# Eight heads in one wave instead of two waves of four, in the inverse of the third mixer's large chunks

## The chip, the cores and the metric

The program runs on one core of a Trainium2 chip, in one launch. The metric is the device time of that launch in microseconds. TensorE, VectorE (DVE), ScalarE (ACT), GpSimd (POOL) and SyncE (SP) each run an instruction stream of their own and meet at semaphores.

## The reference, cut to what matters

The model is two stacks of layers on 256 tokens of width 1024, batch 1. The second stack has four layers on 272 tokens (16 meta tokens and 256 real ones). Its third layer mixes with a gated delta rule over 8 heads of 128, cut into chunks:

```python
def gdn_chunk(state, inputs):
    ...
    lower = jnp.einsum('bhtd,bhsd->bhts', kb, kh) * jnp.exp(jnp.where(strict, diff, -jnp.inf))
    t_mat = jnp.eye(C, dtype=jnp.float32) + lower
    rhs = jnp.concatenate([vb, kb * jnp.exp(b)[..., None]], axis=-1)
    sol = lax.linalg.triangular_solve(t_mat, rhs, left_side=True, lower=True, unit_diagonal=True)
    u, w = sol[..., :GDN_DV], sol[..., GDN_DV:]
    v_new = u - jnp.einsum('bhcd,bhdv->bhcv', w, state)
    attn = jnp.einsum('bhtd,bhsd->bhts', qh, kh) * jnp.exp(jnp.where(incl, diff, -jnp.inf))
    o = attn @ v_new + (qh * exp(b)) @ state
    new_state = state * exp(b_last) + k_dec^T @ v_new
```

(the last two lines are shortened). What the change touches is the solve with the unit lower triangular `t_mat`.

## The kernel before

The kernel is a list of stages. Each stage has a method for each engine (`tensor`, `vector`, `scalar`, `pool`), and these methods are called in the order of the list, so that every engine has one fully unrolled stream. Semaphores count finished instructions by engine; `mark` names a count and `at` waits for it. There is no planner: the order within a stream is the order of the code.

The mixer runs three chunks of 16, 128 and 128 tokens, one after the other, because each needs the state of the one before. The first is a `GdnChunk`, the two large ones (t = 1 and t = 2, the second one with `last` set) are `GdnSquares`. They build the explicit inverse X of `t_mat` and its transpose XT by doubling the block size, seven levels for 128 rows, from 0 to 6. Levels 0 to 4 stay within the four 32x32 squares on the diagonal. These lie "compactly" in tiles of 128 partitions by 8 heads by 32 columns (`Xd`, `XTd`, `Ud`, `BTd`, `LTd`), and a product is a 32x32 matmul on square q of head h. Levels 5 and 6 join the squares and use other tiles.

A level l from 1 to 4 does three sets of 32 products (8 heads by 4 squares) in fp32:

- BX (L4343): the masked part of L times X, into PSUM banks 0 and 1. ScalarE copies it to `Ud` (L4506).
- XB (L4351): X times that, into banks 2 and 3. VectorE subtracts it from `Xd` (L4454).
- XBX (L4354): the transposed product, into banks 4 and 5. VectorE subtracts it from `XTd` (L4455).

The heads are in two groups, g0 with heads 0 to 3 and g1 with heads 4 to 7, one PSUM bank for each group. `square(bank, g, h, q)` is one product's place in PSUM, `squares(bank, g)` the four heads of a group, 128x128. TensorE's order in a level is BX g0, BX g1, then XB and XBX of g0, then XB and XBX of g1. BX of a group waits for that group's X of the level before, XB for that group's copy on ScalarE.

VectorE has other work in its stream ahead of the subtractions of a level: the mask part of the next level (L4412), and what `between(l)` says: the right side less K S (L4430, level 1), the causal mask of the attention (L4433, level 2), pieces of the output's gate (L4442, in the last chunk). ScalarE has in the last chunk one large square (L4508) behind level 1. GpSimd waits for X of level 4 and then copies squares into the tiles of the later levels (L4480). Level 5 is L4361 (BX) and L4366, L4368; level 6 is L4376 and L4382; L4389 is X times the right side, and L4111, L4112 and L4116 the outputs and the new state.

Of the kernel before, what the change touches and what calls it, by code (L numbers as in the profile page):

```python
# [17 lines left out]
ACT = mybir.ActivationFunctionType  # L18
ALU = mybir.AluOpType
AX_X = mybir.AxisListType.X  # L20

P = 128
# [4275 lines left out]
class GdnSquares(GdnChunk):  # L4298
# [7 lines left out]

    def squares(self, bank, g, rows=slice(0, P), width=32):

        return self.c.ps[rows, bank + g, 0:4 * width].rearrange("p (h t) -> p h t", h=4)

    def tensor(self, pe):
# [25 lines left out]
        for l in range(1, self.SMALL):  # L4337
            pe.wait_ge(self.vector_done, self.dve.at("part", l))
            for g, heads in enumerate(self.GROUPS):
                pe.wait_ge(self.vector_done, self.dve.at("X", l - 1, g))  # L4340
                for h in heads:
                    for q in self.Q4:
                        mm = pe.matmul(self.square(0, g, h, q), m["BTd"][l % 2][R[q], h, :], m["Xd"][R[q], h, :], start=True, stop=True)  # L4343
                mm.then_inc(self.tensor_done, self.pe.mark("BX", l, g))
            if l == 1:
                pe.wait_ge(self.vector_done, self.dve.at("AT0"))
            for g, heads in enumerate(self.GROUPS):
                pe.wait_ge(self.scalar_done, self.act.at("BX", l, g))
                for h in heads:
                    for q in self.Q4:  # L4350
                        pe.matmul(self.square(2, g, h, q), m["XTd"][R[q], h, :], m["Ud"][R[q], h, :], start=True, stop=True)  # L4351
                for h in heads:
                    for q in self.Q4:
                        mm = pe.matmul(self.square(4, g, h, q), m["Ud"][R[q], h, :], m["XTd"][R[q], h, :], start=True, stop=True)  # L4354
                mm.then_inc(self.tensor_done, self.pe.mark("XBX", l, g))

        for g, heads in enumerate(self.GROUPS):
            pe.wait_ge(self.vector_done, self.dve.at("X", 4, g))
# [34 lines left out]
    def vector(self, dve):  # L4393
# [14 lines left out]
        def mask(j):  # L4408
            return m["masks"][:, j, :].unsqueeze(1)
# [11 lines left out]
        for g in range(2):  # L4421
            H = slice(4 * g, 4 * g + 4)
            dve.wait_ge(self.tensor_done, self.pe.at("BX", 0, g))
            dve.tensor_tensor(m["Xd"][:, H], mask(0).to_broadcast([P, 4, 32]), self.squares(0, g), ALU.subtract)               .then_inc(self.vector_done, self.dve.mark("X", 0, g))
# [19 lines left out]
        for l in range(1, self.SMALL):  # L4444
# [5 lines left out]
            for g in range(2):  # L4450
                H = slice(4 * g, 4 * g + 4)
                dve.wait_ge(self.tensor_done, self.pe.at("XBX", l, g))
                dve.wait_ge(self.vector_done, self.dve.at("X", l - 1, g))
                dve.tensor_tensor(m["Xd"][:, H], m["Xd"][:, H], self.squares(2, g), ALU.subtract)  # L4454
                dve.tensor_tensor(m["XTd"][:, H], m["XTd"][:, H], self.squares(4, g), ALU.subtract)                   .then_inc(self.vector_done, self.dve.mark("X", l, g))  # L4455
# [15 lines left out]
    def pool(self, pool):  # L4471
# [5 lines left out]
        pool.wait_ge(self.vector_done, self.dve.at("X", 4, 1))  # L4477
# [5 lines left out]
    def scalar(self, act):  # L4483
# [16 lines left out]
        for l in range(1, self.SMALL + 1):  # L4500
            for g in range(2):
                H = slice(4 * g, 4 * g + 4)
                act.wait_ge(self.tensor_done, self.pe.at("BX", l, g))
                if l > 1:
                    act.wait_ge(self.tensor_done, self.pe.at("XBX", l - 1, g))
                act.activation(m["Ud"][:, H], self.squares(0, g), ACT.Copy).then_inc(self.scalar_done, self.act.mark("BX", l, g))  # L4506
# [427 lines left out]
```

## Time and profile before

| what | value |
|---|---|
| median of 3 runs | 2812.64 us |
| lowest and highest | 2811.88 and 2814.21 us |
| the profiled execution's own time | 2804.15 us |
| its span, first to last instruction | 2802.4 us |
| mean granted TensorE clock, as a share of full speed | 0.961 |
| instructions in the trace | 54962 |
| TensorE matmuls, busy | 2606.0 us |
| VectorE busy | 1930.0 us |
| ScalarE busy | 1503.3 us |
| first large chunk, level 1 to the end of level 4 | from 2098.51 to 2119.19 us |
| second large chunk, the same | from 2145.01 to 2165.82 us |

The profile is of one execution. Its times count from the first instruction. A busy time is the sum over instructions that an engine executes; waits and semaphore instructions are not in it. The granted clock of a window is 1.00 at the full 2.4 GHz and 0.50 at 1.2 GHz. "Issue" as a releaser means that the profile shows nothing for which the engine waited. An fp32 product shows as two matmuls and two weight loads.

### The profile page before, as it was taken

Reading aid. Unit: us, or ns where it says so; the run is one execution under the profiler, and the core shown is the slowest. Engines: PE = TensorE matmul, PEld = TensorE weight load, DVE = VectorE, ACT = ScalarE, POOL = GpSimd, SP = SyncE. Lnnn points to the kernel's source line nnn. Section 1 sums busy time; section 2 is a strip of 40 time slices with the busy share of each in tenths; the row PEclk is TensorE's granted clock in tenths of the full one; section 3 lists DMA queues with packets and bytes.
Section 4 is the critical chain, followed back from the end, with each engine's and each line's share of the span. In section 5 each row is a group of like instructions: output and inputs, shape, how many; then the busy total and the mean of one; then the engine's idle time right before and its main releaser. Section 6 shows DMA issues by size and latency. Waiting matters only on the chain.

```text
span 2802.4 us, 54962 instructions
## 1 busy us (share of the span) xinstructions
PE 2606.0 (93%) x21006; PEld 2308.3 (82%) x21006; DVE 1930.0 (69%) x3476; ACT 1503.3 (54%) x2559; POOL 147.7 (5%) x188
## 2 busy tenths in 40 slices
PE   7988899997988999899899998999986899998999
PEld 5845678886776888698799988999886899997999
DVE  3167489997357999775667865777853577766677
ACT  3256378886356888654533464434742433455442
POOL 0010011100001111100000020000010000000000
PEclk9999989999998999999999999999986899999999
DMA  9281389997417999743255433555630255541553
GB/s 324 94 298 61 143 289 380 377 371 271 150 61 266 366 367 358 248 136 106 76 174 171 159 114 106 176 170 165 187 105 3 91 179 167 165 136 62 180 183 118
DMA packets 286595, 529.05 MB, mean 189 GB/s; under 512 B 14336, under 2 KB 207152, under 8 KB 285888
## 3 DMA queue, kind: packets, MB, share of 16 engines
q1 hardware_dynamic: 275472, 506.06, 52.1%
q0 software_dynamic: 9216, 12.61, 1.4%
q10 hardware_dynamic: 1712, 7.69, 0.7%
q8 instruction: 134, 2.20, 0.3%
q14 instruction: 61, 0.50, 0.1%
HBM read 526.21 MB, written 21.06 MB: 195 GB/s over the span
## 4 chain that ended last, share of the span: by engine, by line
PE 77%; DVE 6%; ACT 5%; issue 3%; DMA 1%; PEldq 0%; DVEq 0%; SPq 0%; ACTq 0%; PEld 0%; POOLq 0%
PE ps L2534 17%; PE ps L3116 6%; PE ps L3117 6%; PE ps L3118 6%; PE ps L2137 4%; PE ps L2139 4%; PE ps L2138 4%; PE ps L3136 3%; PE ps L3138 3%; PE ps L3137 3%; PE ps L2173 2%; PE ps L2174 2%; PE ps L2175 2%; PE ps L617 2%; PE ps L1014 1%
## 5 line engine op out<-in xcount | busy, mean ns | idle before, releaser
L2534 PE MATMUL ps<-H_part,W_hi 128*128 128x272 f32 (+2 forms) x2112 | 470.3, 302 | 23.4 <-DVE H_part L2437 11.8
L2339 DVE TENSOR_TENSOR W_lo<-ring,W_hi 128x1024 fp32r<-128x1024 f32 x376 | 443.6, 1222 | 30.1 <-ACT W_hi L2258 29.2
L3165 ACT ACTIVATE W_hi<-ring 128x1024 fp32r<-128x1024 f32 x264 | 263.1, 1049 | 294.3 <-PE ps L3138 185.7
L3116 PE MATMUL ps<-room_part,W_hi 128*128 128x272 f32 (+1 forms) x1408 | 404.7, 287 | 5.0 <-DVE room_part L2437 5.0
L3117 PE MATMUL ps<-room_part,W_hi 128*128 128x272 f32 (+1 forms) x1408 | 403.6, 287 | 0.0
L3118 PE MATMUL ps<-room_part,W_lo 128*128 128x272 f32 (+1 forms) x1408 | 403.0, 286 | 0.0
L2258 ACT ACTIVATE W_hi<-ring 128x1024 fp32r<-128x1024 f32 x376 | 376.6, 1052 | 33.5 <-PE ps L2139 14.2
L2534 PEld LDWEIGHTS ps<-H_part,W_hi 128*128 128x128 f32 x2112 | 351.4, 191 | 41.4 <-issue 29.1
L2534 PE MATMUL ps<-H_part,W_lo 128*128 128x272 f32 (+2 forms) x1216 | 359.2, 295 | 0.0
L3205 DVE TENSOR_TENSOR W_lo<-ring,W_hi 128x1024 fp32r<-128x1024 f32 x264 | 314.2, 1220 | 10.2 <-ACT W_hi L3165 9.4
L2507 DVE TENSOR_TENSOR W_lo<-ring,W_hi 128x1024 fp32r<-128x1024 f32 x186 | 224.6, 1248 | 117.8 <-ACT W_hi L2499 117.2
L3116 PEld LDWEIGHTS ps<-room_part,W_hi 128*128 128x128 f32 x1408 | 265.2, 188 | 7.8 <-issue 7.1
L3117 PEld LDWEIGHTS ps<-room_part,W_hi 128*128 128x128 f32 x1408 | 265.2, 188 | 0.1
L3118 PEld LDWEIGHTS ps<-room_part,W_lo 128*128 128x128 f32 x1408 | 265.1, 188 | 0.0
L3248 DVE TENSOR_TENSOR X<-X,ps 128x272 f32<-128x272 f32 (+1 forms) x352 | 139.4, 431 | 165.1 <-PE ps L3138 162.7
L2499 ACT ACTIVATE W_hi<-ring 128x1024 fp32r<-128x1024 f32 x186 | 185.8, 1050 | 123.3 <-PE ps L2534 84.0
L2534 PEld LDWEIGHTS ps<-H_part,W_lo 128*128 128x128 f32 x1216 | 232.8, 191 | 3.1
L2137 PE MATMUL ps<-W_hi,A_split_hi 128*128 128x512 f32 x512 | 208.8, 408 | 2.8 <-DVE A_split_lo L2345 2.8
L3136 PE MATMUL ps<-room_part,W_hi 128*128 128x272 f32 (+1 forms) x704 | 201.8, 287 | 4.7 <-DVE X L3248 4.7
L2139 PE MATMUL ps<-W_hi,A_split_lo 128*128 128x512 f32 x512 | 202.3, 395 | 0.0
L3138 PE MATMUL ps<-room_part,W_lo 128*128 128x272 f32 (+1 forms) x704 | 202.1, 287 | 0.0
L2138 PE MATMUL ps<-W_lo,A_split_hi 128*128 128x512 f32 x512 | 202.0, 395 | 0.0
(618 smaller groups left out, 5148.7 us busy)
## 6 DMA issues: line engine op xcount, KB each, us to landing
ring<-in_w_expert SPq DMA_DIRECT2D x128, 1024.0 KB, 7.6
ring<-in_w_down SPq DMA_DIRECT2D x108, 1024.0 KB, 6.3
ring<-in_w_gate_up SPq DMA_DIRECT2D x88, 1024.0 KB, 5.1
ring<-in_w_mod SPq DMA_DIRECT2D x42, 1024.0 KB, 5.2
ring<-in_fox_w_in SPq DMA_DIRECT2D x32, 1024.0 KB, 5.9
ring<-in_gdn_w_in SPq DMA_DIRECT2D x16, 1024.0 KB, 5.9
ring<-in_gla_w_in SPq DMA_DIRECT2D x12, 1024.0 KB, 5.2
ring<-in_w_in_even SPq DMA_DIRECT2D x9, 1024.0 KB, 14.4
```

The source lines that it names most:

```text
L2137: pe.matmul(out, xh, wh[:, k, :], start=(q + k == 0), stop=False)
L2138: pe.matmul(out, xh, wl[:, k, :], start=False, stop=False)
L2139: mm = pe.matmul(out, xl, wh[:, k, :], start=False, stop=(q + k == KC - 1))
L2258: act.activation(self.parts(p)[0][:, W], c.ring[:, g % SLOTS, W], ACT.Copy).then_inc(c.hi_done, 1)
L2339: dve.tensor_tensor(lo, c.ring[:, (self.g0 + p) % SLOTS, W], hi.bitcast(F32), ALU.subtract)\
L2534: mm = pe.matmul(self.out(i), a, b, start=(k == 0 and n_part == 0), stop=(k == KC - 1 and n_part == 2))
L3116: pe.matmul(out, wh[:, k, M], hi, start=(k == 0), stop=False)
L3117: pe.matmul(out, wh[:, k, M], lo, start=False, stop=False)
L3118: mm = pe.matmul(out, wl[:, k, M], hi, start=False, stop=(k == KC - 1))
L3136: pe.matmul(out, wh[:, k, M], ah, start=(k == 0), stop=False)
L3138: mm = pe.matmul(out, wl[:, k, M], ah, start=False, stop=(k == 1))
L3205: dve.tensor_tensor(lo, c.ring[:, (self.g0 + p) % SLOTS, C], hi.bitcast(F32), ALU.subtract)\
```

## The change

In `GdnSquares`, levels 1 to 4, the two groups become one wave. TensorE does BX of all heads behind one wait for X of the level before, then XB of all heads behind one wait for ScalarE, then XBX of all heads; XB and XBX have a mark each. ScalarE copies both banks in one instruction for all eight heads, VectorE subtracts both banks from `Xd` behind the mark of XB and from `XTd` behind that of XBX, each in one instruction. A new helper, `all_squares(bank)`, is the view of two banks. Level 0 keeps its two instructions and has one mark for both. Level 5 keeps its groups, but both wait for the whole X of level 4; so does GpSimd.

```diff
+    def all_squares(self, bank):
+
+        return self.c.ps[:, bank:bank + 2, 0:P].rearrange("p a (h t) -> p a h t", h=4)
+
...
         for l in range(1, self.SMALL):
             pe.wait_ge(self.vector_done, self.dve.at("part", l))
-            for g, heads in enumerate(self.GROUPS):
-                pe.wait_ge(self.vector_done, self.dve.at("X", l - 1, g))
-                for h in heads:
-                    for q in self.Q4:
-                        mm = pe.matmul(self.square(0, g, h, q), m["BTd"][l % 2][R[q], h, :], m["Xd"][R[q], h, :], start=True, stop=True)
-                mm.then_inc(self.tensor_done, self.pe.mark("BX", l, g))
+            pe.wait_ge(self.vector_done, self.dve.at("X", l - 1))
+            for h in range(8):
+                for q in self.Q4:
+                    mm = pe.matmul(self.square(0, h // 4, h, q), m["BTd"][l % 2][R[q], h, :], m["Xd"][R[q], h, :], start=True, stop=True)
+            mm.then_inc(self.tensor_done, self.pe.mark("BX", l))
             if l == 1:
                 pe.wait_ge(self.vector_done, self.dve.at("AT0"))
-            for g, heads in enumerate(self.GROUPS):
-                pe.wait_ge(self.scalar_done, self.act.at("BX", l, g))
-                for h in heads:
-                    for q in self.Q4:
-                        pe.matmul(self.square(2, g, h, q), m["XTd"][R[q], h, :], m["Ud"][R[q], h, :], start=True, stop=True)
-                for h in heads:
-                    for q in self.Q4:
-                        mm = pe.matmul(self.square(4, g, h, q), m["Ud"][R[q], h, :], m["XTd"][R[q], h, :], start=True, stop=True)
-                mm.then_inc(self.tensor_done, self.pe.mark("XBX", l, g))
+            pe.wait_ge(self.scalar_done, self.act.at("BX", l))
+            for h in range(8):
+                for q in self.Q4:
+                    mm = pe.matmul(self.square(2, h // 4, h, q), m["XTd"][R[q], h, :], m["Ud"][R[q], h, :], start=True, stop=True)
+            mm.then_inc(self.tensor_done, self.pe.mark("XB", l))
+            for h in range(8):
+                for q in self.Q4:
+                    mm = pe.matmul(self.square(4, h // 4, h, q), m["Ud"][R[q], h, :], m["XTd"][R[q], h, :], start=True, stop=True)
+            mm.then_inc(self.tensor_done, self.pe.mark("XBX", l))
...
         for g, heads in enumerate(self.GROUPS):
-            pe.wait_ge(self.vector_done, self.dve.at("X", 4, g))
+            if g == 0:
+                pe.wait_ge(self.vector_done, self.dve.at("X", 4))
...
-            for g in range(2):
-                H = slice(4 * g, 4 * g + 4)
-                dve.wait_ge(self.tensor_done, self.pe.at("XBX", l, g))
-                dve.wait_ge(self.vector_done, self.dve.at("X", l - 1, g))
-                dve.tensor_tensor(m["Xd"][:, H], m["Xd"][:, H], self.squares(2, g), ALU.subtract)
-                dve.tensor_tensor(m["XTd"][:, H], m["XTd"][:, H], self.squares(4, g), ALU.subtract)                   .then_inc(self.vector_done, self.dve.mark("X", l, g))
+            dve.wait_ge(self.tensor_done, self.pe.at("XB", l))
+            dve.wait_ge(self.vector_done, self.dve.at("X", l - 1))
+            Xd, XTd = (m[x].rearrange("p (a h) t -> p a h t", a=2) for x in ("Xd", "XTd"))
+            dve.tensor_tensor(Xd, Xd, self.all_squares(2), ALU.subtract)
+            dve.wait_ge(self.tensor_done, self.pe.at("XBX", l))
+            dve.tensor_tensor(XTd, XTd, self.all_squares(4), ALU.subtract).then_inc(self.vector_done, self.dve.mark("X", l))
...
-        pool.wait_ge(self.vector_done, self.dve.at("X", 4, 1))
+        pool.wait_ge(self.vector_done, self.dve.at("X", 4))
...
         for l in range(1, self.SMALL + 1):
-            for g in range(2):
-                H = slice(4 * g, 4 * g + 4)
-                act.wait_ge(self.tensor_done, self.pe.at("BX", l, g))
-                if l > 1:
-                    act.wait_ge(self.tensor_done, self.pe.at("XBX", l - 1, g))
-                act.activation(m["Ud"][:, H], self.squares(0, g), ACT.Copy).then_inc(self.scalar_done, self.act.mark("BX", l, g))
+            if l < self.SMALL:
+                act.wait_ge(self.tensor_done, self.pe.at("BX", l))
+                act.activation(m["Ud"].rearrange("p (a h) t -> p a h t", a=2), self.all_squares(0), ACT.Copy)\
+                   .then_inc(self.scalar_done, self.act.mark("BX", l))
+            else:
+                for g in range(2):
+                    H = slice(4 * g, 4 * g + 4)
+                    act.wait_ge(self.tensor_done, self.pe.at("BX", l, g))
+                    act.activation(m["Ud"][:, H], self.squares(0, g), ACT.Copy).then_inc(self.scalar_done, self.act.mark("BX", l, g))
```

## Rows read from the trace of the kernel before

**Rows 1.** The page: span, and busy time of TensorE

```profile
span 2802.4 us, 54962 instructions
...
PE 2606.0 (93%) x21006; PEld 2308.3 (82%) x21006; DVE 1930.0 (69%) x3476; ACT 1503.3 (54%) x2559; POOL 147.7 (5%) x188
```

**Rows 2.** Windows over the levels: busy by engine, clock, DMA share, GB/s

```profile
2098.51:2119.19 20.68, 12.32 (x785) 11.08 (x784) 6.91 (x20) 2.38 (x9) 0.00 (x0) 0.58 0.02 5
...
2145.01:2165.82 20.81, 11.29 (x785) 10.02 (x784) 7.98 (x25) 3.50 (x10) 0.00 (x0) 0.67 0.01 4
```

**Rows 3.** Waits of the whole kernel: us in total, times, longest

```profile
PE ps L4354 <- issue: 11.6, 7, 2.1
...
PE ps L4343 <- issue: 4.6, 3, 1.8
```

**Rows 4.** Timeline at stops: start us, us, operation, count [idle before]

```profile
2100.81 0.17 PEld L4354 LDWEIGHTS ps<-room 32*32 32x32 f32 x6
...
2147.42 0.79 PEld L4343 LDWEIGHTS ps<-room 32*32 32x32 f32 x57 [0.20 <-DVE room L4455]
...
2150.97 0.32 PEld L4354 LDWEIGHTS ps<-room 32*32 32x32 f32 x25
...
2153.54 0.33 PE L4354 MATMUL ps<-room 32*32 32x32 f32 x7 [2.14 <-issue]
```

**Rows 5.** Windows from one resume to the next, five of nine

```profile
2102.18:2106.02 3.84, 1.51 (x128) 1.31 (x129) 1.96 (x4) 0.55 (x2) 0.00 (x0) 0.75 0.02 4
...
2113.01:2117.12 4.11, 2.23 (x127) 1.96 (x128) 0.48 (x2) 0.55 (x2) 0.00 (x0) 0.50 0.02 4
...
2117.12:2120.60 3.48, 2.49 (x129) 2.22 (x129) 0.97 (x4) 0.55 (x2) 1.22 (x4) 0.50 0.02 5
...
2150.07:2153.54 3.47, 1.33 (x128) 1.22 (x128) 0.48 (x2) 0.28 (x1) 0.00 (x0) 0.76 0.02 5
...
2161.14:2164.88 3.74, 1.93 (x128) 1.79 (x128) 0.48 (x2) 0.28 (x1) 0.00 (x0) 0.50 0.02 4
```

**Rows 6.** DMA queues in the window 2144 to 2168

```profile
q8 instruction: 7, 0.11, 1.8%
```

**Rows 7.** A window with one transfer of that queue

```profile
2150.90:2151.30 0.40, 0.40 (x58) 0.39 (x46) 0.35 (x2) 0.00 (x0) 0.00 (x0) 1.00 0.15 41
```

**Rows 8.** Durations by line: ns min/median/max, first and last start, forms

```profile
L4506 ACT ACTIVATE room<-ps x20: 277/277/279, 2099.2 to 2166.5; 128x128 f32<-128x128 f32 x20
...
L4284 ACT ACTIVATE room<-ps x6: 586/597/597, 2074.3 to 2174.9; 128x512 f32<-128x512 f32 x4, 16x512 f32<-16x512 f32 x2
...
L4454 DVE TENSOR_TENSOR room<-room,ps x16: 286/289/289, 2100.8 to 2165.3; 128x128 f32<-128x128 f32 x16
...
L4403 DVE TENSOR_TENSOR H<-ps,room x2: 1225/1225/1225, 2088.8 to 2139.1; 128x1024 f32<-128x1024 f32 x2
```

**Rows 9.** Timeline of level 1 in the second chunk

```profile
2145.01 0.75 PE L4343 MATMUL ps<-room 32*32 32x32 f32 x64
...
2145.54 0.57 ACT L4506 ACTIVATE room<-ps 128x128 f32<-128x128 f32 x2 [2.56 <-PE ps L4343]
...
2145.93 0.34 PEld L4351 LDWEIGHTS ps<-room 32*32 32x32 f32 x29 [0.28 <-issue]
...
2146.21 0.40 PEld L4354 LDWEIGHTS ps<-room 32*32 32x32 f32 x28
```

**Rows 10.** Timeline of the end of level 4, second chunk

```profile
2165.28 0.29 DVE L4454 TENSOR_TENSOR room<-room,ps 128x128 f32<-128x128 f32 x1 [2.41 <-PE ps L4354]
...
2165.49 0.28 DVE L4455 TENSOR_TENSOR room<-room,ps 128x128 f32<-128x128 f32 x1
...
2165.82 0.48 PE L4361 MATMUL ps<-room,H 32*32 32x32 f32 x10 [0.27 <-DVE room L4455]
...
2166.51 0.28 ACT L4506 ACTIVATE room<-ps 128x128 f32<-128x128 f32 x1 [0.64 <-PE ps L4361]
```

**Rows 11.** A window behind the levels of the first chunk

```profile
2119.00:2128.00 9.00, 8.02 (x109) 7.66 (x110) 2.10 (x7) 3.27 (x9) 1.56 (x4) 0.50 0.01 2
```

More of the change, by code:

```diff
@@ L4423, in vector @@
             dve.wait_ge(self.tensor_done, self.pe.at("BX", 0, g))
-            dve.tensor_tensor(m["Xd"][:, H], mask(0).to_broadcast([P, 4, 32]), self.squares(0, g), ALU.subtract)               .then_inc(self.vector_done, self.dve.mark("X", 0, g))
+            ins = dve.tensor_tensor(m["Xd"][:, H], mask(0).to_broadcast([P, 4, 32]), self.squares(0, g), ALU.subtract)
+        ins.then_inc(self.vector_done, self.dve.mark("X", 0))
         dve.tensor_tensor(m["AT"], self.psv(2), m["U"], ALU.mult).then_inc(self.vector_done, self.dve.mark("AT0"))
```

## The prediction

> **What bounds the kernel now.** I read the page first. The program is one core's long chain of matmuls: TensorE is busy 93% of the span and most of the time lies in dense projections that this change does not touch [rows 1]. The third mixer's two large chunks are a small stretch of it. The windows over their inverse levels, from the first product of level 1 to the first products of level 5, come next: 20.68 us in the first chunk (t = 1) and 20.81 us in the second (t = 2), together 41.5 us or 1.5% of the span [rows 2]. To be seen there: the two stretches last the same, though the granted clock is 0.58 in one and 0.67 in the other, and TensorE is busy only 12.3 and 11.3 us of each. Neither TensorE's speed nor its work sets this time.
>
> The list of waits says what does. Over the whole kernel TensorE has idle time that it spends waiting for nothing that the profile shows ("issue"), 11.6 us in 7 pieces before L4354 and 4.6 us in 3 before L4343, and both lines belong to these levels [rows 3]. The pieces are up to 2.1 us long, and they fall inside a row of matmuls of one line where no wait stands: 25 of 32 weight loads of L4354 go out at 2150.97, the other 7 with their matmuls at 2153.54 [rows 4]. So a semaphore cannot be what is missing.
>
> The next view fixes it. Cut the time at the moments at which TensorE goes on after such a piece (I call them resumes): each stretch holds 128 weight loads and 128 matmuls, within one or two missing records, whatever they are and at either clock, and lasts 3.47 to 4.11 us, though TensorE is busy for 1.3 to 2.5 us of it [rows 5], which shows five of the nine. An fp32 product is two matmuls and two loads here (the 32 of BX show as 64 [rows 9]). In the window 2144 to 2168 an "instruction" queue has 7 transfers of 0.11 MB together, so 16 KB each, which is 64 bytes for each of 256 instructions, and one is seen in the window from 2150.90, 0.8 us behind the resume at 2150.07 and over 2 us ahead of the next at 2153.54 [rows 5 to 7]. I read this as instruction fetch: a block of 256 TensorE instructions is asked for when the block before it is entered, and can run some 3.5 us later. A block of long matmuls hides that. A block of 32x32 matmuls, 0.0134 us apart at half clock, is eaten in 1.93 us when nothing waits (the stretch from 2161.14; with a last matmul of 0.24, since 7 take 0.33 [rows 4, 5]), and then TensorE stands.
>
> The Trainium skill says the contrary of this (Runtime: NRT & Kernel Launch, Instruction fetch mechanics): the next page of 256 instructions is fetched during the current one, and that is hidden because issue is slower than the fill. This trace does not agree [rows 4 to 7]: the block size is the same, the hiding is not. By that rule the gaps would be something else and the waits between engines would decide, which is the second rival below.
>
> **The change, part by part.** The level l = 1 to 4 was BX (g0, g1), XB and XBX of g0, XB and XBX of g1, each 16 products; it becomes BX of all 32, XB of all 32, XBX of all 32.
>
> TensorE's instructions: 96 products a level before and after, at the same tiles and sizes. Of the waits, those for the mask part and for X stand on one semaphore and the trace shows no instruction of their own for them. So I take TensorE's count of instructions, and with it the places of the block borders in its stream, as unchanged; the fetch prices them at 3.47 to 4.11 us a block, mean 3.68 over the five stretches of the first chunk from 2102.18 to 2120.60, and 3.70 over the four of the second from 2150.07 to 2164.88 [rows 5].
>
> ScalarE: two evictions of 128x128 at 0.277 us become one of 128x256. Between 0.277 for 128 and 0.597 for 512 elements [rows 8] a straight line gives 0.277 + 0.320 x 128/384 = 0.384 us. Saved 0.17 us a level, 1.4 us over eight. VectorE: four subtractions (0.29 and 0.28 us, starting 0.2 us apart [rows 8, 10]) become two of 128x256, each by the line from 0.289 (128) to 1.225 us (1024) [rows 8]: 0.289 + 0.93 x 128/896 = 0.42 us. A pair of groups took 2 x (0.2 + 0.28) = 0.96 and takes 0.84: saved 0.12 a level, 1.0 us over eight. Bounds for the wide form over two banks, which no row shows: not below one narrow one, 0.28, and not above two, 0.56. Eight waits of 21 ns go with them; nothing is queued behind. All of this lies under the fetch: it is worth 0 as long as a block's own time stays under 3.47 us.
>
> What it adds is exposed waiting. Before, ScalarE evicted g0 while TensorE did BX of g1, and VectorE did g0 during the products of g1. Now TensorE stops for the whole trip twice a level. ScalarE's trip: last matmul 0.24, start 0.07 (g0's half of the 64 ends about 2145.47, its eviction starts at 2145.54), eviction 0.38, weight load 0.12 (2145.82 to 2145.93 [rows 9]), 0.81 us. VectorE's trip: 0.24 + 0.07 + 0.42 + 0.05 (2165.77 to 2165.82 [rows 10]) = 0.78 us, the subtraction from Xd being hidden under XBX. A block that holds both trips needs 1.69 (128 pairs to the last start: 1.93 less 0.24) + 0.81 + 0.78 = 3.28 us, under the shortest stretch, 3.47. By counting 192 pairs a level from the observed borders, three of the nine blocks hold both trips (cover left 0.2 us each), and the others one (cover 1 us) but the last of the first chunk, which has level 5's eviction too and is worked out below. If that cover is gone, the excess is paid in full: with both trips 0.3 us dearer it would be 3 x 0.1 us. I take 0 for it, and up to +1 for the range.
>
> The first chunk: its first border of the levels lies at pair 166 of 192 in level 1 (6 loads into g1's XBX at 2100.81 [rows 4]: 64 + 3 x 32 + 6), so the block before it is entered at pair 38, in BX, ahead of any wave that changes. So its resumes stay, up to the last at 2120.60, which lies in level 5's products behind all of the change. The new order reaches that border sooner than 2120.60: resume at 2117.12, 26 + 64 pairs to 2118.4, VectorE's trip to 2119.1, level 5's first 32 pairs and an eviction to 2120.0. Its 0.77 us gap shrinks to 0.6. Sum of the chunk: 0.
>
> The second chunk: its first resume is 2150.07, in BX of level 2 at pair 57 [rows 4], so its block is entered 128 pairs earlier, at pair 121 of level 1: in XBX of g0 before, at about 2146.46 (24 loads behind 2146.21 [rows 9]), which is 3.6 us before the resume, and this is the length of a fetch again. Afterwards pair 121 is the 57th of XB, and XB waits for the whole wave: BX ends at 2145.76, ScalarE 2145.83 to 2146.21, first load 2146.33, 57th pair 0.54 us later: 2146.87. So the block is entered 0.4 us later, and every resume of this chunk with it: +0.4. At its end, 7 pairs behind the last resume, 0.33 us lie from the resume to the last of them, as before; then one wide subtraction (0.42) stands where two narrow ones took 0.49, and level 5, whose g0 used to go ahead of X of g1 (only g1's waits until 2165.82 [rows 10]), starts as one piece after it. ScalarE's second eviction then queues behind its first: 2165.82 + 0.4 - 0.1 for the first products, + 0.5 to the first eviction, + 0.28 to the second, + 0.28 to its end, against 2166.51 + 0.28 before, 0.69 behind the first products: +0.6 in all for the chunk, against +0.4 from the entry alone. GpSimd's copies, which wait for X of level 4, come at the same offset, and L4389, which waits for the last, starts 3 us behind it. I take +0.5.
>
> Sum: 0 + 0.5 = +0.5 us. The profiled execution took 2804.15 us (span 2802.4 and 1.75 around it), so 2804.65; the median of the three runs shown, 2812.64, lies 8.49 us above it, and nothing here bears on that difference: **2813.1 us**.
>
> **Rivals.**
> 1. Wide instructions gain (faster side). The Trainium skill (VectorE: DVE Perf Modes, The TRN2 errata) says that a fixed cost is paid per instruction, so that few wide ones win. As a mechanism here: if the idle time were the engines' own instruction time, the 1.4 + 1.0 us saved above would come off: 2810.2. If in addition the gaps came from having two waves, and half of the 16.2 us went [rows 3], 8.1 more: 2802.1. For it: the time is spent idle, not in work. Against: the gaps stand inside rows of matmuls with no wait. 3% for the large one; the small one, 5%, is still within no change.
> 2. Lost overlap is paid (other side). If the gaps are not tied to a count of instructions, or grow with the level, TensorE's idle time in each level is the two trips without the last matmuls' own 0.24, 0.57 + 0.54, against the 0.27 us for which it waited for VectorE before [rows 10]: 0.84 us more, eight times 6.7: 2819.3. It decides from where a trip costs over 0.2 us more than I priced it. For it: nothing in the rows shows how the fetch behaves with long waits inside a block. 7%.
> 3. The clock. The granted clock is 0.75 and 0.76 in the stretches from 2102.18 and 2150.07 and 0.50, the lower level, in the last stretch of both chunks [rows 5]. The dense products behind the levels are what pays: 8.0 us busy at 0.50 in the first chunk, of which full clock would take off up to 4 [rows 11], and what follows at the upper level would pay as much if the rise came later. A rise that moves by 3 us costs or gives about 3. For it: the idle pieces move within the blocks. Against: their count and sum hardly change. 11%, half to each side: 2810 to 2816.
> 4. The change does nothing: the end of each chunk is as before, 2812.6. 10%.
>
> **How the numbers follow.** The forecast (2812.2 to 2814.2 by the spread of its terms) has 64%, rivals as given. A measurement of this kernel can tell about 0.2%, 5.6 us, from no change. Faster by more: the large part of rival 1 and a little of the clock, 4%. Slower by more: rival 2 and a little of the clock, 8%. Within: 88%. The range leaves out both large rivals and holds the clock's cases: 2809.0 to 2817.0.
>
> **What the profile of the changed kernel would show.** The resumes still 128 pairs and 3.5 to 4.1 us apart, issue gaps inside rows of matmuls and shorter by the new waits; the first chunk's levels 20.7 us again; the second's about 21.2; ScalarE's eviction near 0.38 and VectorE's subtraction near 0.42 us, eight and sixteen of them; the transfers of the instruction queue as many as before. It is wrong if the distance between resumes changes with the waves: longer by a trip, the fetch starts on something other than the entry of a block; shorter, the gaps were waits.

## The result, and the profile after

The changed kernel took 2813.99 us (median of 12 runs, 2810.12 to 2818.24) against 2806.85 us for the kernel before (12 runs, 2802.81 to 2814.21). The ratio is 1.0023 with a 95% interval of 1.0013 to 1.0032, so by the ratio the change made the kernel slower by 6.4 us (3.6 to 9.0). Run again later, beside 32 new runs of the kernel before, its ratio was 1.0005 (0.9993 to 1.0017), +1.4 us (-2.0 to +4.8). The two intervals share the stretch from +3.6 to +4.8 us. The totals of one kernel spread over 10 us from run to run, so the levels are read from the traces below, and the totals stand beside them.

The page of the changed kernel, the span and the busy times of the engines:

```profile
span 2809.2 us, 54914 instructions
...
PE 2608.6 (93%) x21006; PEld 2311.0 (82%) x21006; DVE 1928.8 (69%) x3460; ACT 1501.8 (53%) x2551; POOL 147.5 (5%) x188
```

TensorE's count of matmuls and loads is the same and its busy time grew by 2.6 us, while the span grew by 6.8 us [rows 1].

The windows over the levels of the changed kernel (length, busy time and count for each engine, granted clock, DMA share, GB/s). The first two reach from the first BX of level 1 to the first product of level 6, the last two only to the first product of level 5:

```profile
2100.80:2126.10 25.30, 15.06 (x849) 13.15 (x849) 6.79 (x14) 2.35 (x7) 1.56 (x4) 0.56 0.01 4
...
2152.13:2176.10 23.97, 13.56 (x850) 11.86 (x849) 8.24 (x19) 3.41 (x8) 1.80 (x4) 0.64 0.02 4
...
2100.80:2123.61 22.81, 12.73 (x770) 11.14 (x769) 6.40 (x12) 1.53 (x4) 0.00 (x0) 0.57 0.02 4
...
2152.13:2173.97 21.84, 11.47 (x769) 9.97 (x768) 7.47 (x17) 2.59 (x5) 0.00 (x0) 0.65 0.02 4
```

The same windows of the kernel before, and two that begin at BX of level 0 and are needed further down:

```profile
2098.52:2121.62 23.10, 13.95 (x849) 12.47 (x849) 7.30 (x22) 3.04 (x11) 1.56 (x4) 0.57 0.02 4
...
2145.01:2167.41 22.40, 12.75 (x849) 11.29 (x848) 8.93 (x27) 4.09 (x12) 1.40 (x3) 0.65 0.02 5
...
2091.29:2121.62 30.33, 18.42 (x928) 16.60 (x929) 9.91 (x28) 6.50 (x25) 1.56 (x4) 0.60 0.02 4
...
2141.58:2167.41 25.83, 15.48 (x928) 13.79 (x928) 11.53 (x33) 5.49 (x18) 1.40 (x3) 0.70 0.02 5
```

From BX of level 1 to level 6 the first chunk went from 23.10 to 25.30 us and the second from 22.40 to 23.97: +2.2 and +1.6, together +3.8 us. To level 5 it was 22.81 and 21.84 us where [rows 2] have 20.68 and 20.81. The second profile of the changed kernel has 25.55 and 24.30 us, +2.45 and +1.90, together +4.35. Both sums lie in what the two intervals of the total share. The profiles differ as much elsewhere: the first chunk's levels begin 2.3 us later in the changed kernel's, and the stretch from them to the second chunk's is another 2.6 us longer, with a lower granted clock. Neither place runs changed work. The second of them, in the kernel before and in the changed kernel:

```profile
2121.62:2145.01 23.39, 19.74 (x216) 18.97 (x216) 10.50 (x32) 8.09 (x20) 0.43 (x1) 0.86 0.01 2
...
2126.10:2152.13 26.03, 22.39 (x216) 21.61 (x217) 10.48 (x32) 8.08 (x20) 0.43 (x1) 0.77 0.01 2
```

The same 216 matmuls are busy 2.65 us longer at 0.77 than at 0.86, which is the whole difference.

TensorE's idle time without a visible releaser, of the whole changed kernel (total, times, longest):

```profile
PE ps L4357 <- issue: 4.8, 4, 1.8
...
PE ps L4353 <- issue: 3.5, 3, 1.3
...
PE ps L4346 <- issue: 3.3, 3, 1.2
```

With [rows 3] beside it: 11.6 us of such gaps in 10 pieces where 16.2 us in 10 pieces stood before. The gaps did shrink. The levels grew all the same, so the gaps are no account of what can be gained.

The stretches from one resume to the next, as in [rows 5]:

```profile
2104.39:2109.24 4.85, 2.46 (x127) 2.09 (x128) 1.89 (x3) 0.38 (x1) 0.00 (x0) 0.50 0.01 3
...
2109.24:2113.27 4.03, 2.23 (x128) 1.99 (x127) 1.18 (x3) 0.00 (x0) 0.00 (x0) 0.50 0.01 4
...
2113.27:2117.02 3.75, 2.24 (x129) 1.97 (x129) 0.42 (x1) 0.38 (x1) 0.00 (x0) 0.50 0.02 4
...
2117.02:2121.60 4.58, 2.46 (x127) 2.09 (x128) 0.42 (x1) 0.38 (x1) 0.00 (x0) 0.50 0.02 4
...
2161.25:2165.91 4.66, 2.38 (x127) 2.03 (x128) 1.34 (x5) 0.38 (x1) 0.00 (x0) 0.50 0.02 4
...
2169.63:2173.10 3.47, 2.15 (x128) 1.89 (x129) 0.42 (x1) 0.38 (x1) 0.00 (x0) 0.50 0.02 5
```

Each still holds 128 pairs of load and matmul, within a missing record. But three of the nine (there are five in the first chunk and four in the second) are 4.85, 4.58 and 4.66 us long, and the others are 3.47 to 4.03. What is special about the three is in the timeline of the first of them:

```profile
2104.39 0.50 PEld L4357 LDWEIGHTS ps<-room 32*32 32x32 f32 x26 [1.29 <-issue]
...
2105.06 0.42 DVE L4460 TENSOR_TENSOR room<-room,ps 128x256 f32<-128x256 f32 x1 [1.72 <-PE ps L4357]
...
2105.60 0.97 PEld L4346 LDWEIGHTS ps<-room 32*32 32x32 f32 x64 [0.71 <-DVE room L4460]
...
2106.76 0.38 ACT L4508 ACTIVATE room<-ps 128x256 f32<-128x256 f32 x1 [4.78 <-PE ps L4346]
...
2107.20 0.75 PE L4353 MATMUL ps<-room 32*32 32x32 f32 x37 [0.49 <-ACT room L4508]
...
2109.24 0.58 PE L4353 MATMUL ps<-room 32*32 32x32 f32 x26 [1.29 <-issue]
```

The block is entered at 2104.39 and its first 26 pairs go out. Then TensorE waits for VectorE, and BX of level 2 starts at 2105.60. A transfer of the instruction queue, some 1.0 to 1.6 us behind the entry in the other blocks, is seen only in the window from 2106.70:

```profile
2106.70:2107.10 0.40, 0.01 (x2) 0.00 (x0) 0.25 (x1) 0.34 (x1) 0.00 (x0) 0.50 0.15 41
```

Narrower windows put its start between 2106.85 and 2106.90. That is 2.5 us behind the entry, 1.3 us behind the first load after the wait (2105.60), and 2.4 us ahead of the resume at 2109.24. The wait for X is an instruction of its own in TensorE's sequencer, the part of the engine that passes instructions on. Of two waits that the code puts ahead of one instruction, the later one shows so in these traces; the other shows no instruction and is, by this reading, attached to the weight load. The wait for X is an instruction of its own in the kernel before too, where it waits for the first group alone and ends early. The line of that wait in the changed kernel, and in the kernel before (times, duration, first and last start):

```profile
L4343 PEldq EVENT_SEMAPHORE  x8: 51/51/51, 2097.3 to 2167.6; - x8
```

```profile
L4340 PEldq EVENT_SEMAPHORE  x8: 51/51/51, 2094.9 to 2158.0; - x8
```

The first chunk's +2.2 us is all in these stretches. The second chunk's +1.6 is not: its four stretches take 15.87 us where four took 14.81, and 3.00 us lie between its last resume (2173.10) and level 6 where 2.53 did (from 2164.88), +0.5 for the end of the levels. The kernels below that make X in one wave have 2.96 to 3.01 us there, also where no stretch is long, and those that keep its groups 2.50 to 2.54 (but for the run with fewer pairs, whose last resume lies elsewhere). So this part belongs to the change and not to the long stretches. What remains is 0.04 us at its start.

### The profile page after: what moved, and what is told of

Read it like the earlier page. It is cut to its first block, busy times and chain, and to the rows that moved or that the text cites. A ratio compares the mean times of both kernels' runs of the same rounds, so it can differ in the third digit from the quotient of the medians.

```text
span 2809.2 us, 54914 instructions
## 1 busy us (share of the span) xinstructions
PE 2608.6 (93%) x21006; PEld 2311.0 (82%) x21006; DVE 1928.8 (69%) x3460; ACT 1501.8 (53%) x2551; POOL 147.5 (5%) x188
## 4 chain that ended last, share of the span: by engine, by line
PE 77%; DVE 6%; ACT 5%; issue 3%; DMA 1%; DVEq 0%; PEldq 0%; SPq 0%; ACTq 0%; POOLq 0%; PEld 0%
PE ps L2534 18%; PE ps L3116 6%; PE ps L3117 6%; PE ps L3118 6%; PE ps L2137 4%; PE ps L2139 4%; PE ps L2138 4%; PE ps L3136 3%; PE ps L3138 3%; PE ps L3137 3%; PE ps L2173 2%; PE ps L2174 2%; PE ps L2175 2%; PE ps L617 2%; PE ps L997 1%
```

## The experiments

The figures for the levels are the time from the first BX of level 1 to the first product of level 6. The stretches and the starts of transfers below are read from each run's trace, the same way as above. Theory W says that the request for the next block of instructions is held while TensorE's sequencer stands at a wait of its own; theory T says that the exposed trips to ScalarE and VectorE cost by themselves.

| kernel | levels, first chunk | second chunk | ratio of the total (95%) |
|---|---|---|---|
| before | 23.10 | 22.40 | 1 |
| changed | 25.30 | 23.97 | 1.0023 (1.0013 to 1.0032) |
| changed, again | 25.55 | 24.30 | 1.0005 (0.9993 to 1.0017) |
| changed, waits in the other order | 23.39 | 22.71 | 1.0015 (1.0000 to 1.0030) |
| changed, one wait less | 23.86 | 22.96 | 1.0006 (0.9991 to 1.0022) |
| before, late wait | 24.15 | 23.53 | 1.0003 (0.9987 to 1.0019) |
| before, BX twice | 31.30 | 30.03 | 1.0056 (1.0037 to 1.0074) |
| BX wave alone | 23.07 | 22.77 | 0.9999 (0.9989 to 1.0010) |
| X wave alone | 25.10 | 23.44 | 1.0014 (1.0004 to 1.0024) |
| before, one wait less | 23.09 | 22.63 | 0.9991 (0.9982 to 1.0001) |

**The waits in the other order.** The changed kernel with one edit:

```diff
-            pe.wait_ge(self.vector_done, self.dve.at("part", l))
             pe.wait_ge(self.vector_done, self.dve.at("X", l - 1))
+            pe.wait_ge(self.vector_done, self.dve.at("part", l))
```

> The changed kernel with the two waits ahead of BX in levels 1 to 4 in the other order (X first, then the mask part). Same instructions, same count. In the changed kernel the wait for X is an instruction of its own at TensorE's sequencer, 8 times, and the stretches between resumes that begin shortly before it are 4.0 to 4.8 us where the others are 3.5 to 4.0. Theory W (the request for the next block of instructions cannot go out while the sequencer stands at a wait of its own; a wait attached to a weight load does not hold it): now the wait for the mask part, long fulfilled, is the one of its own, all stretches are 3.5 to 4.1 us again, and the time from the first BX of level 1 to the first product of level 6 falls from 25.3 and 24.0 us (first and second chunk) to about 23.1 and 22.9. Theory T (a block's own time with two trips in it decides, whichever way it waits): nothing moves, 25.3 and 24.0 within 0.5.

Measured: 23.39 and 22.71 us. With the same instructions in number and kind, 1.9 of the 2.2 us and 1.3 of the 1.6 us are gone. Windows over both chunks' levels, over two stretches, and one with a transfer:

```profile
2096.29:2119.68 23.39, 15.03 (x849) 13.03 (x849) 6.79 (x14) 2.36 (x7) 1.56 (x4) 0.57 0.02 4
...
2143.45:2166.16 22.71, 13.59 (x850) 11.80 (x849) 8.24 (x19) 3.42 (x8) 1.80 (x4) 0.66 0.02 4
...
2100.13:2103.70 3.57, 2.45 (x129) 2.05 (x129) 1.89 (x3) 0.38 (x1) 0.00 (x0) 0.50 0.02 5
...
2103.70:2107.05 3.35, 2.23 (x129) 1.96 (x128) 1.18 (x3) 0.00 (x0) 0.00 (x0) 0.50 0.02 5
...
2101.30:2101.70 0.40, 0.40 (x32) 0.40 (x36) 0.40 (x2) 0.00 (x0) 0.00 (x0) 0.50 0.15 41
```

The timeline of the block that took 4.85 us in the changed kernel, entered here at 2100.13:

```profile
2100.13 0.50 PEld L4357 LDWEIGHTS ps<-room 32*32 32x32 f32 x26 [1.53 <-issue]
...
2100.80 0.42 DVE L4460 TENSOR_TENSOR room<-room,ps 128x256 f32<-128x256 f32 x1 [1.97 <-PE ps L4357]
...
2101.27 0.94 PEld L4346 LDWEIGHTS ps<-room 32*32 32x32 f32 x64 [0.65 <-DVE room L4460]
...
2103.70 0.44 PEld L4353 LDWEIGHTS ps<-room 32*32 32x32 f32 x25 [0.23 <-issue]
```

The engine waits as before, 26 pairs into the block, until 2101.27. But the transfer starts at 2101.41, 1.3 us behind the entry, not 2.5, and the stretch takes 3.57 us with both trips in it. The other two blocks that were long take 3.85 and 3.57 us here. So a block with both trips runs at the fetch's pace, and what cost was the kind of the wait. Theory T falls as the main cause. The total, 1.0015, does not tell these apart: its interval reaches from no change to +8 us.

**One wait less.** The changed kernel without the wait for the mask part, which VectorE has done ahead of X:

```diff
-            pe.wait_ge(self.vector_done, self.dve.at("part", l))
             pe.wait_ge(self.vector_done, self.dve.at("X", l - 1))
```

> The changed kernel without the wait for the mask part in levels 1 to 4 (VectorE has done that part ahead of X, whose mark is later on the same semaphore). Eight instructions fewer, none of the waits an instruction of its own but the two of level 1 for the attention. Theory W: as with the waits in the other order, about 23.1 and 22.9 us from BX of level 1 to level 6, total 3 us under the changed kernel. Theory T: 25.3 and 24.0, total unchanged.

Measured: 23.86 and 22.96 us. 1.4 and 1.0 us gone, on the side of W, 0.5 us less than with the other order in the first chunk. Its stretches there are 3.47, 4.02, 3.74, 4.02 and 3.75 us, against 3.57, 3.35, 3.74, 3.85 and 4.01, so the 0.5 lies in the spread of undisturbed stretches.

**The late wait alone.** The kernel before, in which only the wait changes:

```diff
-                pe.wait_ge(self.vector_done, self.dve.at("X", l - 1, g))
+                pe.wait_ge(self.vector_done, self.dve.at("X", l - 1, 1))
```

> The kernel before, with one edit: BX of the first group waits for X of the second group too, as an instruction of its own, and nothing else is merged. Theory W: that wait now ends only after the last subtraction of the level, 0.9 us later than before, in the blocks that have it within their first pairs (three of the first chunk's, two of the second's); each is longer by 0.3 to 0.9 us: 23.1 and 22.4 us become 24.5 and 23.3. Theory T (only a block with both long trips exceeds the fetch; here ScalarE's work stays overlapped): 23.1 and 22.4 within 0.4.

Measured: 24.15 and 23.53 us, +1.05 and +1.13 with nothing merged and ScalarE's copies still overlapped; three blocks were held where five had been expected. The timeline of the first long block, and the windows of it, of the next one, and of a transfer:

```profile
2103.70 0.50 PEld L4354 LDWEIGHTS ps<-room 32*32 32x32 f32 x26 [1.41 <-issue]
...
2104.97 0.97 PEld L4343 LDWEIGHTS ps<-room 32*32 32x32 f32 x64 [0.78 <-DVE room L4455]
...
2108.34 0.49 PE L4354 MATMUL ps<-room 32*32 32x32 f32 x20 [1.56 <-issue]
```

```profile
2103.70:2108.34 4.64, 2.41 (x127) 2.08 (x128) 1.96 (x4) 0.55 (x2) 0.00 (x0) 0.50 0.01 4
...
2108.34:2111.89 3.55, 2.23 (x129) 1.99 (x129) 1.31 (x5) 0.28 (x1) 0.00 (x0) 0.50 0.02 5
...
2105.90:2106.30 0.40, 0.40 (x35) 0.31 (x27) 0.40 (x1) 0.25 (x2) 0.00 (x0) 0.50 0.16 41
```

The transfer comes, at 2106.03, 2.3 us behind the entry and 1.1 behind the end of the wait at 2104.97. The stretches are 4.64, 3.55, 3.47, 4.64, 3.47 us in the first chunk and 3.74, 5.01, 3.51, 3.47 in the second. The three long ones begin 26, 26 and 7 pairs ahead of the wait. In the blocks where the wait lies some 71 or 90 pairs in, the request is out by then, and they keep 3.5 us.

How far into a block such a wait must stand is not settled by the pairs alone. In level 1 the wait for ScalarE is an instruction of its own too (L4350 in the changed kernel). In the first chunk it stands 26 pairs behind a border that TensorE passes without a stop, and ends at about 2102.07; the transfer starts at 2102.05 and was not held. No run explores this.

**BX twice.** The kernel before with each product of BX issued two times:

```diff
-                for h in heads:
+                for h in list(heads) * 2:
```

> The kernel before with every product of BX in levels 1 to 4 issued twice into the same place (the result is the same): 64 more pairs of load and matmul a level, 256 a chunk, two blocks of 128. If instruction fetch paces the levels, each 128 pairs cost a stretch of 3.5 to 4.1 us: +7.4 us a chunk, the time from BX of level 1 to level 6 becomes 30.5 and 29.8, total +14.8. If TensorE's own time or the waits between engines pace them, 64 pairs cost 0.7 to 0.9 us a level: +3.2 us a chunk, total +6.5.

Measured: 31.30 and 30.03 us, +8.2 and +7.6, and the total +15.7 us (10.4 to 20.8).

```profile
2100.99:2132.29 31.30, 17.17 (x1105) 15.87 (x1105) 7.30 (x22) 3.05 (x11) 1.56 (x4) 0.55 0.02 4
...
2155.56:2185.59 30.03, 15.99 (x1105) 14.56 (x1105) 8.92 (x27) 4.10 (x12) 1.41 (x3) 0.61 0.02 5
...
2108.70:2112.17 3.47, 1.93 (x128) 1.80 (x128) 0.00 (x0) 0.56 (x2) 0.00 (x0) 0.50 0.02 5
```

256 pairs a chunk are two blocks, and they cost two stretches (the instruction queue has 8 transfers in the first chunk's window instead of 6), though a block of them is 1.93 us of work without any wait in it (the last window: 3.47 us, ScalarE twice, VectorE not once). TensorE's busy time grew by 3.2 us in each chunk. This shows that the levels are paced by the count of instructions, 0.03 us for each pair, and not by TensorE's work or by the trips. That it is their fetch is read from the transfer that goes with each block.

**Half the change: BX in one wave.** ScalarE's wide copy on the kernel before, the waits for X as they were:

```diff
-                pe.wait_ge(self.scalar_done, self.act.at("BX", l, g))
+                pe.wait_ge(self.scalar_done, self.act.at("BX", l))
```

> One half of the change alone: the kernel before, but ScalarE copies BX of all eight heads in one instruction and both groups' XB wait for it; XB, XBX and VectorE stay in groups, and the wait for X that is an instruction of its own is still the early one, of the first group. Theory W (a late wait of its own delays the next request for instructions): this half costs nothing in the stretches; in the first chunk 23.1 us from BX of level 1 to level 6 as before, in the second 22.4 + 0.4, since its first block of the levels is entered later. Theory T (each exposed trip costs): half of the change's cost, 24.2 and 23.2 us.

```profile
2101.75:2124.82 23.07, 14.74 (x850) 12.84 (x849) 7.31 (x22) 2.36 (x7) 1.56 (x4) 0.57 0.02 4
...
2148.76:2171.53 22.77, 14.03 (x850) 12.13 (x849) 8.92 (x27) 3.42 (x8) 1.40 (x3) 0.59 0.02 4
```

Measured: 23.07 and 22.77 us. The first chunk pays nothing and the second 0.37 us, all of it ahead of its first resume, where the prediction has the later entry of the first block. The total is unchanged, 0.9999.

**The other half: X in one wave.** XB and XBX of all heads, VectorE's wide subtractions and the one late wait, BX and ScalarE in groups:

> The other half alone: the changed kernel, but BX and ScalarE's copies by groups as before; XB and XBX of all heads, VectorE's wide subtractions and the one late wait for X stay. Theory W: nearly the whole cost of the change, 24.8 to 25.3 and 23.5 to 24.0 us from BX of level 1 to level 6. Theory T: half of it, 24.2 and 23.2 us.

```profile
2096.13:2121.23 25.10, 14.90 (x850) 13.13 (x849) 6.79 (x14) 3.04 (x11) 1.56 (x4) 0.56 0.02 4
...
2147.39:2170.83 23.44, 13.27 (x850) 11.67 (x849) 8.24 (x19) 4.10 (x12) 1.80 (x4) 0.64 0.02 4
...
2100.05:2104.63 4.58, 2.41 (x127) 2.09 (x128) 1.89 (x3) 0.56 (x2) 0.00 (x0) 0.50 0.01 4
```

Measured: 25.10 and 23.44 us, +2.0 and +1.0, of the change's 2.2 and 1.6. The third window is a block with the own wait near its head: 4.58 us. Its other two held blocks take 4.86 and 4.67. The two halves sum to 2.0 and 1.4 us.

**The changed kernel again.**

> The changed kernel once more, for a second profile and more times beside the same runs of the kernel before. From BX of level 1 to level 6 the first profile has 25.3 and 24.0 us against 23.1 and 22.4 before, +3.8 together, and the measured total is +0.23%, 6.4 us. If the 2.6 us that the levels do not explain are spread by the clock and the state of the rest of the run, the stretches repeat within 0.5 us and the total difference comes nearer to 4 us; if they belong to the change, it stays at 6 to 7.

Measured: 25.55 and 24.30 us, within 0.35 us of the first profile; the same three blocks take 5.13, 4.86 and 4.39 us. The total came out at +1.4 us, under the +4 of the levels. So the 2.6 us that the levels did not explain the first time are not a steady part of the change. In this profile the levels begin at 2098.46 and the stretch between the chunks' levels takes 23.86 us at a granted clock of 0.85, where the first had 26.03 at 0.77. Of the other runs without K S among the levels, only the X wave alone shows the long stretch, 26.16 us at 0.77; the rest have 23.3 to 23.9 us at 0.84 to 0.87. Why the clock returned later in these two is not shown.

**K S among the levels.** If TensorE stands between fetches, long products that now lie ahead of the levels can go there. The kernel before, with two edits for TensorE and VectorE's subtraction moved from level 1 to level 4:

```diff
-        for h in range(8):
-            mm = pe.matmul(self.head(6, h, P), m["KBE"][:, h, T], m["S"][:, h, :], start=True, stop=True)
...
         for l in range(1, self.SMALL):
-            pe.wait_ge(self.vector_done, self.dve.at("part", l))
...
+            for h in {1: range(0, 3), 2: range(3, 6), 3: range(6, 8)}.get(l, ()):
+                mm = pe.matmul(self.head(6, h, P), m["KBE"][:, h, T], m["S"][:, h, :], start=True, stop=True)
```

> A version made from what the runs say. The kernel before without the wait for the mask part (so no late or early wait of its own in levels 2 to 4), and with the eight 128x128 products K S, which stand ahead of level 1 and are waited for there, issued behind BX in levels 1 to 3 (three, three, two) and subtracted by VectorE in level 4. They need 3.7 us of TensorE in the first chunk and 2.0 in the second, and TensorE waits 2.8 and 0.7 us for ScalarE ahead of them. If the levels are paced by the fetch, these products fit into the idle pieces, the time from the first BX of level 0 to the first product of level 6 falls by 4 to 6 us in the first chunk (30.3 before) and 2 to 3 in the second (25.8 before), and the total is 5 to 9 us under the kernel before. If the levels are paced by TensorE's work and the waits, the products only change places: the gain is the wait ahead of them, at most 3.5 us together.

Measured: 2800.57 us, ratio 0.9968 (0.9957 to 0.9979), 9.0 us under the kernel before (5.9 to 12.1) and faster than both kernels. The windows from BX of level 0 to level 6:

```profile
2092.02:2118.33 26.31, 18.29 (x929) 16.12 (x929) 9.84 (x28) 6.31 (x25) 1.56 (x4) 0.61 0.02 4
...
2138.59:2164.28 25.69, 16.21 (x929) 14.22 (x929) 11.44 (x33) 5.51 (x18) 1.40 (x3) 0.71 0.02 5
```

The first chunk went from 30.33 to 26.31 us, -4.0 as expected. The second went from 25.83 to 25.69, where 2 to 3 us had been expected. There, by this reading, the eight products had covered one fetch: in the new order its first resume is already at 2143.33 and six resumes lie in the window where five were. The gain was given back as one more exposed block. The whole mixer, from the first product of the first large chunk to the projection behind it, took 105.30 us against 110.48. So 5.2 us of the 9.0 are located in it, and the rest is not.

**The control for it.** The kernel before without the wait for the mask part:

> The kernel before without the wait for the mask part in levels 1 to 4, so that none of its waits for X is an instruction of its own; the control for the version with K S among the levels. The own wait for the first group's X ends early there, so theory W gives it little: 22.8 to 23.2 and 22.1 to 22.5 us from BX of level 1 to level 6 (23.1 and 22.4 before), total within 1 us of before. If much of the 9 us that the version gained came from this edit, it shows here.

Measured: 23.09 and 22.63 us, ratio 0.9991. In the groups' order the own wait costs nothing that can be seen, and what the version gained came from K S.

**The waves with K S among the levels.**

> The changed kernel (one wave of eight heads) without the wait for the mask part and with K S among the levels. Whether the waves are worth anything once the two costs found are taken away. From BX of level 0 to the first product of level 6 the version in groups has 26.3 and 25.7 us. Theory W with a fetch-paced stream: the same within 1 us, total 0 to 2 us above the version in groups (2800.6, 7 us under the kernel before). If the exposed trips cost by themselves there, 0.8 us a level: 3 us more in each chunk.

Measured: 26.88 and 25.73 us from BX of level 0 to level 6, +0.6 and 0.0 over the groups, ratio 0.9972 (0.9960 to 0.9984). With both costs gone, one wave or two is the same within the 0.6 us of the first chunk. No gain by the wide instructions is seen, and the 3 us a chunk that exposed trips would have cost by themselves are not there.

**Fewer pairs.**

```diff
-                    for q in self.Q4:
+                    for q in (range(3) if l == 4 else self.Q4):
```

> The version with K S among the levels, without XB of the fourth square in level 4 (8 products; nothing reads X of that square afterwards, so the output is unchanged; VectorE's subtraction reads what level 3 left there). 16 pairs of load and matmul fewer in each chunk, an eighth of a block. If the fetch sets the price, -0.46 us a chunk on average (0.2 to 0.5 by where the last border falls); if TensorE's work does, -0.2 us. Total about 1 us under the version, which the times cannot tell and the stretches may.

Measured: 26.22 and 23.78 us, -0.1 and -1.9, and a ratio of 0.9986 (0.9975 to 0.9998), above the version's 0.9968. The window of the second chunk gained four times what 16 pairs are priced at, and the total did not follow. This run settles nothing.

## Why the prediction was right or wrong

- The range held the median, 2813.99 in 2809.0 to 2817.0 with 2813.1 as the forecast, but that was luck. The three runs of the kernel before that were shown lie at its upper end (2812.64, against 2806.85 over twelve). The forecast difference was +0.5 us and the measured one +6.4 in the first comparison and +1.4 in the second, about +4 in the traces. "Within 0.2%" had 88% and the first ratio is just outside it, the second within.
- The pace by blocks of 256 instructions was right, and it is shown by the run with BX twice (+15.8 us in the levels for four blocks) and by 128 pairs in every stretch shown.
- The step that failed is the sentence on TensorE's waits, "the trace shows no instruction of their own for them". The trace of before shows eight, of 51 ns. The conclusion drawn from it, an unchanged count of instructions and unchanged borders, held. But the wait that stands alone was the wait for X, and the change turned it from an early into a late one. With it falls the unconditional claim that a block is asked for when the one before it is entered. It is asked for then if the sequencer does not stand at a wait of its own. Three blocks in nine had the wait 26, 27 and 7 pairs behind their entry and cost 4.85, 4.58 and 4.66 us where 3.47 to 4.11 were priced. That is the sign of being wrong that the prediction named itself: stretches longer by a trip, so that the fetch starts on something other than the entry of a block. Attaching that wait to the load took back 1.9 of 2.2 and 1.3 of 1.6 us.
- "First chunk: 0" was therefore +2.2 (again: +2.45). "Second chunk: +0.5" was +1.6 (again: +1.9). Once the own wait is gone the levels are near what was priced: +0.3 and +0.3 with the waits in the other order, +0.0 and +0.4 with the BX wave alone. The parts of the second chunk's +0.5 were less right than their sum. Its first resume, which was to come 0.4 us later (5.06 us behind BX of level 1 before), came at 5.10 and 5.97 in the two profiles of the changed kernel, 5.85 with the waits swapped and 5.43 with the BX wave alone: 0.4 is inside this scatter, and not shown by it. The end of the levels, taken at 0.1 to 0.2, was +0.5 (3.00 against 2.53 us).
- The prices of the wide instructions were right: 0.384 us for ScalarE's copy against 0.383 measured, 0.42 for VectorE's subtraction against 0.422. So was the cover: a block with both trips ran in 3.57 us. The lines by source of the changed kernel:

```profile
L4508 ACT ACTIVATE room<-ps x8: 383/383/383, 2101.6 to 2170.0; 128x256 f32<-128x256 f32 x8
...
L4458 DVE TENSOR_TENSOR room<-room,ps x8: 420/422/422, 2102.9 to 2171.6; 128x256 f32<-128x256 f32 x8
```

- Rival 1, a gain by wide instructions, did not come: with the own wait gone the changed kernel's levels are still 0.3 us above before, and the waves with K S are no faster than the groups. A fixed cost per instruction is there (one wide copy takes 0.383 us, two narrow ones 2 x 0.277), but it is paid on engines that wait for the fetch. Rival 2 had the right side and, in the first comparison, the right size. As a mechanism it was wrong but for its last sentence, that no row showed how the fetch behaves with long waits inside a block. What I should have asked is which instruction each wait is attached to. Rival 3, the clock, did show in the first profile: 2.65 us more in the dense products behind the first chunk's levels, at 0.77 against 0.86. It did not show in the second.
- The Trainium skill's statement that fetch is hidden (Runtime: NRT & Kernel Launch, Instruction fetch mechanics) was weighed and set aside. The trace of the run with BX twice does not agree with it either: a block of 128 pairs that needs 1.93 us lasts 3.47.

## What to carry to other kernels

Where TensorE runs hundreds of small matmuls, look first for idle pieces inside one line's row of matmuls and count the instructions between them; if the count is always the same, the stream is paced by its instruction fetch. Each further block then costs a whole fetch (BX twice), long products moved in between can be covered (4.0 us gained in one chunk, 0.1 in the other), and wider evictions gain nothing. That fewer small products gain is to be expected but not shown here: the one run for it settled nothing. Of two waits ahead of one instruction, the one written last becomes an instruction of its own: let it be the one that is long fulfilled, or leave it out where the other implies it. When work is moved out of a stretch in which it hid a fetch, count the blocks again, because the next fetch becomes visible.

## What the runs showed of the hardware that was not expected

- A wait of its own in TensorE's sequencer, met 7, 26 or 27 pairs into a block that TensorE has just entered after a stop, holds back the transfer of the next block. In the twelve such blocks of four traces (the changed kernel twice, the late wait alone, the X wave alone) it starts 1.0 to 1.6 us behind the end of the wait (2.0 to 2.6 behind the entry), and in the three blocks of the swapped order, where the same wait is attached to a load, 1.2 to 1.3 us behind the entry. TensorE resumes 2.2 to 3.0 us behind the transfer in both cases.
- An attached wait is also a little shorter: ahead of the first load behind VectorE's subtraction TensorE's loads stood idle for 0.71 us with the wait of its own and 0.65 us with the attached one, in the timelines above.
- The fp32 32x32 products cost 0.03 us a pair of load and matmul in such a stretch (+8.2 and +7.6 us for 256 pairs, at a mean granted clock of 0.55 and 0.61), while their own spacing is 0.0133 us at half clock (64 of BX in 1.08 us, the last one 0.24).
